# A two-layer hybrid diffusion step with an expert mixture: gate products among key transposes, another order of the routing, and one expert transfer with a place of its own

## What is computed

```python
def block(x, mod, lp, ctx=None):
    sh1, sc1, g1, sh2, sc2, g2 = jnp.split(mod, N_MOD, axis=-1)
    h = rmsnorm(x, lp['norm1_g']) * (1 + sc1) + sh1
    y, new = token_mixing(h, lp, ctx)        # pooling, banded attention, latent attention; gated, merged, projected
    x = x + g1 * y
    h = rmsnorm(x, lp['norm2_g']) * (1 + sc2) + sh2
    x = x + g2 * ec_moe(h, lp['w_router'], lp['w_gate'], lp['w_up'], lp['w_down'])
    return x, new

def ec_moe(h, w_router, w_gate, w_up, w_down):
    b, n, d = h.shape
    cap = CAPACITY_FACTOR * n // N_EXPERTS   # 16 slots for the prompt, 32 for the latents, 16 experts
    aff = jax.nn.softmax(jnp.einsum('bnd,de->ben', h, w_router), axis=1)
    vals, idx = lax.top_k(aff, cap)
    xg = jax.vmap(lambda hb, ib: hb[ib])(h, idx)
    a = jnp.einsum('becd,edf->becf', xg, w_gate)
    u = jnp.einsum('becd,edf->becf', xg, w_up)
    o = jnp.einsum('becf,efd->becd', jax.nn.silu(a) * u, w_down) * vals[..., None]
    return jax.vmap(lambda ib, ob: jnp.zeros((n, d), ob.dtype).at[ib.reshape(-1)].add(ob.reshape(-1, d)))(idx, o)
```

## Time and profile before

| what | value |
|---|---|
| median of 3 runs | 1815.55 us (1815.0 to 1815.77) |
| the profiled execution | 1816.19 us |
| its span on the core | 1814.3 us |
| TensorE busy | 1702.5 us, 94% |
| VectorE, ScalarE, GpSimd busy | 650.5, 288.4, 118.5 us |
| DMA | 533.81 MB, mean 294 GB/s |
| expert transfers | 192 of 2048 KB, 31.6 and 30.6 us from issue to landing |
| granted TensorE clock, mean | 0.998 |

### The profile page before, as it was taken

How to read it: one execution, slowest core, us unless ns; L and a number is a source line. 1 busy time by engine, 2 the same in 40 slices (tenths; PEclk the granted TensorE clock), 3 DMA queues, 4 the chain that set the end, 5 groups by cost and what they waited for, 6 DMA issues and landing times.

```text
span 1814.3 us, 18937 instructions
## 1 busy us (share of the span) xinstructions
PE 1702.5 (94%) x7152; PEld 801.6 (44%) x7152; DVE 650.5 (36%) x1381; ACT 288.4 (16%) x733; POOL 118.5 (7%) x160
## 2 busy tenths in 40 slices
PE   6998999999999998898899989999999999988987
PEld 2455566654434333242245555666543433323322
DVE  1345655567212210221124466555661221211211
ACT  2233322111100010000022432221021000000000
POOL 1151000000000000000012500000000000000000
PEclk9999999999999999999999999999999999999999
DMA  9430333754899999999983213337648999999997
GB/s 383 178 122 24 116 116 116 278 200 182 356 429 432 431 430 432 430 431 429 429 359 119 99 47 116 116 128 294 234 189 359 429 430 431 431 431 431 430 431 315
DMA packets 49106, 533.81 MB, mean 294 GB/s; under 512 B 5840, under 2 KB 6896, under 8 KB 10384
## 3 DMA queue, kind: packets, MB, share of 16 engines
q1 hardware_dynamic: 45776, 524.39, 69.8%
q0 software_dynamic: 2112, 7.97, 1.2%
q10 hardware_dynamic: 1152, 0.56, 0.1%
HBM read 530.76 MB, written 2.13 MB: 294 GB/s over the span
## 4 chain that ended last, share of the span: by engine, by line
PE 72%; DMA 23%; DVE 3%; ACT 1%; issue 1%; SPq 0%; ACTq 0%; POOL 0%; DVEq 0%; POOLq 0%
PE bank L1957 21%; DMA ring<-in_w_moe 21%; PE bank L1583 12%; PE bank L1602 7%; PE bank L1648 6%; PE bank L1994 5%; PE bank L1819 5%; PE bank L1684 2%; DMA ring<-in_w_mix 2%; PE bank L1886 2%; PE bank L1745 2%; PE bank L1611 1%; PE bank L1720 1%; PE bank L1626 1%; PE bank L1571 1%; PE bank L1574 1%
## 5 line engine op out<-in xcount | busy, mean ns | idle before, releaser
L1583 PE MATMUL bank<-hT,ring 128*128 128x384 f32 x768 | 258.6, 490 | 0.0
L1957 PE MATMUL bank<-M,hT 128*64 128x512 f32 x1024 | 228.8, 595 | 21.0 <-DMA M<-in_w_moe 19.8
L1957 PE MATMUL bank<-ring,hT 128*64 128x512 f32 x1024 | 227.2, 595 | 11.4 <-DMA ring<-in_w_moe 11.4
L1583 PEld LDWEIGHTS bank<-hT,ring 128*128 128x128 f32 x768 | 143.4, 190 | 103.4 <-issue 7.8
L1957 PEld LDWEIGHTS bank<-M,hT 128*64 128x64 f32 x1024 | 72.5, 137 | 167.8 <-issue 136.8
L1957 PEld LDWEIGHTS bank<-ring,hT 128*64 128x64 f32 x1024 | 72.2, 137 | 158.2 <-issue 139.7
L1602 PE MATMUL bank<-M,ring 128*128 128x384 f32 x384 | 134.6, 494 | 5.6 <-ACT M L760 5.6
L1957 PE MATMUL bank<-ring,M 128*64 128x512 f32 x512 | 115.4, 596 | 18.7 <-DMA ring<-in_w_moe 18.7
L1957 PE MATMUL bank<-M 128*64 128x512 f32 x512 | 115.7, 595 | 12.3 <-DMA M<-in_w_moe 12.3
L1648 PE MATMUL bank<-ring,hT 128*128 128x512 f32 (+1 forms) x288 | 117.4, 567 | 2.8 <-DVE hT L1051 2.1
L951 ACT ACTIVATE hT<-bank 128x512 f32<-128x512 f32 x32 | 19.1, 598 | 571.6 <-PE bank L1957 571.6
(11 more groups left out here) (236 smaller groups left out, 1536.8 us busy)
## 6 DMA issues: line engine op xcount, KB each, us to landing
M<-in_w_moe SPq DMA_DIRECT2D x96, 2048.0 KB, 31.6
ring<-in_w_moe SPq DMA_DIRECT2D x96, 2048.0 KB, 30.6
ring<-in_w_mix SPq DMA_DIRECT2D x110, 1024.0 KB, 5.1
ring<-in_w_mix SPq DMA_DIRECT2D x4, 576.0 KB, 4.9
modrow<-in_bias_rows POOLq DMA_DIRECT2D x4, 512.0 KB, 5.7
g2slot<-in_bias_rows POOLq DMA_DIRECT2D x4, 512.0 KB, 7.3
M<-in_counts POOLq DMA_DIRECT2D x2, 768.0 KB, 12.4
out<-x SPq DMA_DIRECT2D x6, 256.0 KB, 2.0
```

Of the source, the lines that this page charges most:

```text
L1583: ins = mm(ps[:, 0:TOK], w[:, q, (j % 4) * P:(j % 4 + 1) * P], hT[:, 4 * h + q, :], start=(h == 0 and q == 0), stop=(h == 1 and q == 3))
L1957: ins = mm(bank[b][64 * e:64 * e + 64, :], lhs(e, 4 * h + q), w[:, q, :], start=(h == 0 and q == 0), stop=(h == 1 and q == 3))
```

## The change

It has four parts. First, `wq` products run tile by tile with both halves, in other banks; ScalarE issues the cache stores after the evacuation of `tq`; key transposes `tkm` get other banks, and `gate(0, 0)` stands between the second and third of them, its tanh ahead of the first exponentials. Head pair 0 is written out: both branch products, the second gate and the transposed probabilities follow in a new order, and VectorE merges the first branch ahead of its first `divide`. Second, `column(6)` to `column(8)` come at head pairs 2, 4 and 6 instead of 3, 5 and 7. Third, routing: `turned(0, 0)` moves from VectorE to ScalarE, `router_part(0)` ahead of `normal_x(2)`, `route(0)` ahead of the last gate row, and bank 2's gather ahead of `turn_slots(1)`. Fourth, the small arrays move into one buffer `arena` of two units; once attention and most of routing have read them, transfer j = 16 of the last group (pair 7, its transfer 4) is loaded there, right behind the ring's first fill, and the ring's own transfer is left out. The order of unit pairs becomes 0, 4, 2, 6. `wrout` is cleared at each layer's start.

```diff
@@ -30 @@
 EARLY = (8, 10, 12)
-DOUBLES = EARLY + (0, 2, 4, 6) + (14,)
+DOUBLES = EARLY + (0, 4, 2, 6) + (14,)
 ND = len(DOUBLES)
@@ -139 @@
         for t in range(T):
-            use(("wq", h, t), 1 + 3 * h + t)
+            use(("wq", h, t), 1 + 2 * t + h)
     for g in range(4):
@@ -150 @@
         for h in range(2):
-            use(("tkm", t, h), ((3, 4), (5, 0), (7, 4), (1, 2))[t][h])
+            use(("tkm", t, h), ((7, 0), (3, 4), (3, 4), (5, 6))[t][h])
     for m in range(NM):
...
             use(("sb", m, j), 2 * j + 1)
-        if m in (3, 5, 7):
-            use(("col", 6 + (m - 3) // 2), 5)
+        if m in (2, 4, 6):
+            use(("col", 5 + m // 2), 5)
         for j in range(2):
@@ -229 @@
 LANDED = [sum(slot_of(u) == s for u in UNITS) for s in range(RINGX)]
-LANDS = [c + (12 * NP // ND if s % 2 == 0 else 0) for s, c in enumerate(LANDED)]
+LANDS = [c + (12 * NP // ND - (s == DOUBLES[16 % ND]) if s % 2 == 0 else 0) for s, c in enumerate(LANDED)]
 SUMMED = (6, 7, 8, 9, 4, 5, 10, 11)
@@ -268 @@
         ring = sb("ring", [P, RING, UNIT])
-        kT = sb("kT", [P, 512])
+        M = sb("M", [P, 20160])
+        arena = sb("arena", [P, 2 * UNIT])
+        kT = arena[:, 1024:1536]
         cols = sb("cols", [P, L, NCOL])
-        rows = sb("rows", [P, NROW])
+        rows = arena[:, 1536:1536 + NROW]
         const = sb("const", [P, NCONST])
         cs = sb("cs", [P, KB, 32])
-        modrow = sb("modrow", [P, 2, 512])
+        modrow = arena[:, 0:1024].rearrange("p (a b) -> p a b", b=512)
         shift = [sb(f"shift{k}", [P, KB, 2]) for k in range(2)]
...
         g2slot = sb("g2slot", [P, D])
-        wrout = sb("wrout", [P, KB, 32])
-        kr = sb("kr", [P, 4, ROPE])
-        krg = sb("krg", [P, 4, ROPE])
+        wrout = arena[:, 3016:3272].rearrange("p (a b) -> p a b", b=32)
+        kr = arena[:, 3272:3400].rearrange("p (a b) -> p a b", b=ROPE)
+        krg = arena[:, 3400:3528].rearrange("p (a b) -> p a b", b=ROPE)
         sskr = sb("sskr", [P, 4])
@@ -287 @@
         rcon = sb("rcon", [P, 2, NE])
-        wrA = sb("wrA", [P, 2, KB, 32])
+        wrA = arena[:, 2504:3016].rearrange("p (s a b) -> p s a b", a=KB, b=32)
         negsink = sb("negsink", [P, SH])
@@ -296 @@
 
-        M = sb("M", [P, 20160])
 
@@ -379 @@
         landed = [sem(f"landed{s}") for s in range(RINGX)]
+        resident_in = sem("resident_in")
         first_half_used = sem("first_half_used")
@@ -547 @@
 
-            def load_group(l, gr, first):
+            def load_resident(l):
+
+                wait_full(sp, l, ("rpart", 0))
+                wait_full(sp, l, ("modb", 10, 0))
+                sp.dma_start(arena[:, :], a["w_moe"][l, NP - 1, 4]).then_inc(resident_in, 16)
+
+            def load_group(l, gr, first, last=False):
                 for j in range(len(EARLY) if first else 0, 24):
                     s = DOUBLES[j % ND]
+                    if last and j == 16:
+                        continue
+                    if first and j == ND:
+                        load_resident(l)
                     if j >= ND:
@@ -576 @@
                 load_group(l, 0, True)
-                with sp.Fori(1, NG) as gr:
+                with sp.Fori(1, NG - 1) as gr:
                     load_group(l, gr, False)
+                load_group(l, NG - 1, False, True)
             for n in range(2):
@@ -591 @@
             step(nc.gpsimd.memset(mhalf[:, :], -0.5))
-            nc.gpsimd.memset(wrout[:, :, :], 0.0).then_inc(pads_zero, 1)
             events = [0]
@@ -602 @@
             for l in range(L):
-                if l == 0:
-                    pool.wait_ge(pads_zero, 1)
-                else:
+                if l > 0:
                     x_final(pool, l - 1)
+                nc.gpsimd.memset(wrout[:, :, :], 0.0).then_inc(pads_zero, 1)
+                pool.wait_ge(pads_zero, l + 1)
                 loads = [
@@ -802 @@
 
-                for dst, src, s in ((outs[2][0, l], ktok[:, 0, :], ktok_ready), (outs[3][0, l], vtok[:, 0, :], None),
-                                    (outs[4][0, l], ckvtok[:, 0, :], ckvtok_ready), (outs[5][0, l], kr[:, 0, :], None)):
-                    if s is not None:
-                        act.wait_ge(s, 3 * l + 1)
-                    act.dma_start(dst, src).then_inc(cache_out, 16)
-
                 for t in range(T):
@@ -826 @@
                     read(l, ("tq", t), F(qT[:, :, t * P:(t + 1) * P], ps[:, :].rearrange("p (b t) -> p b t", t=P), ACT.Copy))
+
+                for dst, src, s in ((outs[2][0, l], ktok[:, 0, :], ktok_ready), (outs[3][0, l], vtok[:, 0, :], None),
+                                    (outs[4][0, l], ckvtok[:, 0, :], ckvtok_ready), (outs[5][0, l], kr[:, 0, :], None)):
+                    if s is not None:
+                        act.wait_ge(s, 3 * l + 1)
+                    act.dma_start(dst, src).then_inc(cache_out, 16)
 
@@ -852 @@
 
+                gate_tanh(l, 0, 0)
                 for j in range(2):
@@ -863 @@
                     for j in range(2):
-                        gate_tanh(l, (2 * m + j) // 8, (2 * m + j) % 8)
+                        if m:
+                            gate_tanh(l, (2 * m + j) // 8, (2 * m + j) % 8)
+                        elif j == 0:
+                            gate_tanh(l, 0, 1)
                         if j == 0 and m not in (0, 4):
@@ -916 @@
                 expert_exp(2)
+                turned(0, 0)
                 wait_full(act, l, ("wo", 1, 0))
...
                 turned(0, 1)
+                router_part(0)
                 normal_x(2)
-                router_part(0)
                 expert_exp(0)
@@ -1298 @@
                 for m in range(NM):
+                    if m == 0:
+                        merge(l, 0, 0)
                     for j in range(2):
                         divide(l, m, j)
-                    if m in (3, 5, 7):
-                        column(6 + (m - 3) // 2)
-                    merge(l, m // 4, 2 * m % 8)
+                    if m in (2, 4, 6):
+                        column(5 + m // 2)
+                    if m:
+                        merge(l, m // 4, 2 * m % 8)
                     for j in range(2):
...
                             sum_rows(6 + m // 2, m % 2, (0, 1))
-                    merge(l, m // 4, 2 * m % 8 + 1)
+                            if m == 0:
+                                merge(l, 0, 1)
+                    if m:
+                        merge(l, m // 4, 2 * m % 8 + 1)
                     if m + 1 < NM:
@@ -1427 @@
                 number(P, TOK)
-                turned(0, 0)
                 add_mixed(1, 0)
@@ -1711 @@
                     wait_read(pe, l, ("tkc", t))
-                for h in range(2):
-                    arrived(l, ("wq", h, 0))
-                    w = ring[:, slot_of(("wq", h, 0)), 0:3 * QR].rearrange("p (k n) -> p k n", n=QR)
-                    for t in range(T):
+                    for h in range(2):
+                        arrived(l, ("wq", h, 0))
+                        w = ring[:, slot_of(("wq", h, 0)), 0:3 * QR].rearrange("p (k n) -> p k n", n=QR)
                         ps = begin(l, ("wq", h, t))
@@ -1748 @@
 
-                for t in range(4):
+                for t in range(2):
+                    turn_heads("tkm", t, 3 + t)
+                gate(l, 0, 0)
+                for t in (2, 3):
                     turn_heads("tkm", t, 3 + t)
@@ -1756 @@
                     wait_read(pe, l, ("pool", g))
+
                 def column(i):
@@ -1777 @@
                     b, j = m // 4, 2 * m % 8
+                    if m == 0:
+                        branch(l, 0, 0)
+                        gate(l, 0, 1)
+                        turn_probs(l, 0, 0)
+                        branch(l, 0, 1)
+                        turn_probs(l, 0, 1)
+                        scores(l, 1)
+                        continue
                     gate(l, b, j)
-                    if m not in (0, 4):
+                    if m != 4:
                         values(l, m - 1)
-                    if m in (3, 5, 7):
-                        column(6 + (m - 3) // 2)
+                    if m in (2, 4, 6):
+                        column(5 + m // 2)
                     branch(l, b, j)
@@ -1926 @@
                 router(0)
+                route(0)
                 gate_row(11, 1)
-                route(0)
                 pe.wait_ge(xn2_ready, 3 * l + 2)
...
                 turn_affinities(1, 0, 1)
-                gather_sample(0, (1,))
+                gather_sample(0, (1, 2))
                 turn_slots(1, 0, 1)
-                gather_sample(0, (2, 3))
+                gather_sample(0, (3,))
                 pe.wait_ge(xn2_ready, 3 * l + 3)
@@ -1950 @@
                         s = DOUBLES[j % ND]
-                        pe.wait_ge(landed[s], 16 * (l * LANDS[s] + LANDED[s] + gr * (24 // ND) + j // ND + 1))
+                        resident = last and j == 16
+                        if resident:
```

(7 more changed lines are left out.)

## The result

The changed kernel took 1797.46 us (median of 4 runs, 1796.35 to 1798.8) against 1815.66 (4 runs, 1815.0 to 1816.09) beside it: a ratio of 0.9901 (95% interval 0.9885 to 0.9916), 18.2 us less. The forecast was 1790.9: the sign and the range held, and the kernel came out 6.6 us above it.

A forecast was written before the change was run, and what follows sets the result against it. Transfers bound the expert stages, TensorE attention and routing. Per layer 5.4 (attention) + 2.9 (routing) + 4.9 (resident transfer), twice 26.4, less 1.7 for a clock fall: 24.7 us saved, median 1790.9 us, range 1785.7 to 1799.

The forecast's parts named there:

- Attention, up to the third gate product: Attention: TensorE waits of 8.1 us per layer go, a new 2.7 comes; net 5.4 per layer, bounds 3 to 6.3.
- The stores: Attention's cache stores: issued later, they take 5.2 us to land, still before the first key/value evacuation; no cost.
- The new wait: Attention, before the second gate: TensorE idles 2.7 us per layer until VectorE's merge frees bank 7.
- the clock fall behind it: After the 2.7 us idle before the second gate: one fall counted in the two layers, costing 1.7 us.
- The column products: Attention, one head pair earlier: may wait up to 0.6 us, cover other small tanh waits (2.0 in two layers); net 0.
- Rival (c): Second gate in attention: its wait grows, clock falls in both layers, 1.5 us more idle each; 1795.6 us, chance 0.10.
- Routing: Between attention and experts: 0.5 us from earlier logits plus 2.4 from fewer gather records, 2.9 per layer, bounds 1.5 to 3.3.
- Resident transfer: Expert stage: one transfer leaves the stream, loaded while DMA would be idle; 4.9 us per layer, bounds 0 to 5.3.
- Rival (d): Expert stream: new memory places lower its rate; slower than before under 417.6 GB/s, 1832.7 us at 410; chance 0.03.
- The signs listed as wrong: Transfer rate under 425 GB/s, first reuse waiting behind the resident transfer, or experts starting under 6 us earlier.
- the experts' start in layer 0: Sign of success: layer 0's expert products start 8.3 us earlier, near 458.6 us.
- the end of layer 0's stream: Sign of success: layer 0's expert stage is over 13 us earlier.

The follow-up runs named there:

- the kernels with the early merge: Changed kernel with the first merge between the two first maxima and columns back at head pairs 3, 5, 7: 1788.88 us; with M also at its old address: 1783.86 us.
- the two edits of before: Kernel before with small arrays in the arena, nothing loaded there, M behind: 1821.9 us; kernel before with M directly behind the ring: 1819.05 us.
- the last kernel: Changed kernel with the first merge between the first maxima, columns back at head pairs 3, 5, 7, and M at its old address: 1783.86 us, ratio 0.9823.

## Why the prediction was right, and where it was not

**Attention, up to the third gate product: right, and too small.** The waits that were to go went. From the start of the last transposes ahead of `wq` (`tq`) to the start of the third gate product before had 112.81 to 178.92 and after 113.79 to 173.07, 6.8 us less; the idle listed in between fell from 8.06 in seven waits to 2.55 in one, only 5.5. The other 1.3 hangs on the waits too. Groups without a wait between them overlap in the timeline. PE, layer 0, before:

```profile
139.53 1.04 PE L1739 MATMUL bank<-const,M 128*96 128x128 f32 x8
140.40 3.60 PE L1745 MATMUL bank<-ring,M 128*128 128x512 f32 x8
```

The first ends, by the profile, 0.17 after the second starts. Behind a wait there is no such overlap, so each of the six waits that went gave some 0.16 beyond its listed idle, 1.0 in all. The last 0.3 is in groups that were listed longer behind a wait (3.70 against 3.60 for a key/value product, 1.08 against 1.04 for a key transpose).

The stores landed in 1.7 us where the earlier trace rows has 5.2; that size was wrong and cost nothing. DMA issues of after:

```profile
out<-arena ACTq DMA_DIRECT2D x2, 16.0 KB, 1.7
```

In before the DMA engines were busy with other transfers while the stores were under way (a share of 0.91 to 1.02 from 110 to 116 us in layer 0); in after the first store went out at 115.3, and from 116 to 118 us the share was 0.51. The Trainium skill (DMA: Bandwidth & Descriptors, Anatomy of one DMA) gives about 2 us as the fixed cost of a transfer issued by GpSimd. These stores are ScalarE's; the row of after is near that figure, and that of before is not.

**The new wait: right** (2.55 for 2.7), and so was the clock fall behind it: in after it came in one of the two layers, and it cost 1.6 for 1.7.

**The column products: wrong at nothing.** The wait of up to 0.6 was in the bounds (0.67), but the step "they cover the other small tanh waits: 0" missed the clock. Behind the short wait and the 1.9 us of one-column products it fell in both layers of after, 1.6 us each. The two were not tried apart, but neither was followed by a fall alone: none came behind the column products of after at head pairs 4 and 6, which had no wait, nor behind the 0.65 us wait of the kernels with the early merge. Without falls attention would have given 6.9 and 7.0 per layer, 1.5 more than the forecast 5.4; three falls of 1.6 took 4.8 of 13.9, and 9.1 is left. That this equals the forecast 2 x 5.4 - 1.7 is luck: a gain that was put too small and two falls that were not foreseen cancel. Rival (c) has its falls here, but in another place than it said.

**Routing: right, in sum and in its parts** (2.80 and 2.99 for 2.9). In layer 0 the slot transposes came 55.21 us after the output projection's start instead of 55.67, 0.5 as forecast, and 8 records of 1.13 stand behind them instead of 16 of 3.55, the forecast 2.4. Of these 2.4, 1.5 is the clock (3.55 against 2.05 in the layer in which it held); before pays that in some executions only.

**Resident transfer: right** at 5.0 for 4.9, a price that was read straight off the stream.

**The rate: the step that failed.** Rival (d) named the mechanism, M starting elsewhere, and priced only the size at which it would turn the sign, under 417.6 GB/s; for the sum it counted nothing, "nothing in the rows". What the runs show in the place of that nothing is 0.6%, 431 to 428 GB/s, 2.4 us per layer (428.9 against 426.5), 4.8 in all. The signs listed as wrong ("under 425") would not have caught it either. A cost that no row shows should have had both ends in the sum: each 1% on the 857 us of streamed transfers is 8.6 us, a third of the whole forecast. Of the signs, the experts' start in layer 0 came 7.1 us earlier (466.92 to 459.79) for the forecast 8.3, and the end of layer 0's stream 9.7 earlier (898.25 to 888.51), where over 13 had been named: that sign failed, by the rate and by the program's start.

The account against the forecast, profile to profile: 24.7 forecast, 19.25 measured. Experts 9.8 - 5.1 = 4.7 short (rate 4.8), attention and routing 0, the start of the program 1.0, the rest -0.2. That start goes with M's address too, at least in part, since DMA is never idle there: from 6 to 40 us it moved 410 to 412 GB/s in the five profiled executions that have M at its old address and 403 to 406 in the nine others. In executions without a clock fall at the start, the first long group begins at 46.0 to 46.7 with M at its old address and at 46.8 to 47.2 with M elsewhere; in four others the clock fell there, and it begins at 47.8 to 49.0. The last 1.1 us to the medians is that the forecast took before's median as 0.64 below its profile, while after's is 0.52 above.

**Left open.** Why M's address matters is not known: two other addresses were held against the old one (directly behind the ring, and 2272 bytes above the old), and no alignment or boundary was tested by itself. In the built programs M starts at byte 145920 of a partition where the stream runs at 431 GB/s, a multiple of 512; the addresses with 428, 118912 and 148192, are no multiples of 256. That is the property to try first. In the two edits of before other arrays moved with M, though none that the stream writes; in the last kernel the small arrays stay away from their old places and the rate is back, which speaks for M alone.

## What to carry to other kernels

In a stage that streams without a gap, compare the rate to three digits before and after any edit of the memory layout, and put an array that the stream fills back at its old address before you judge the edit; 0.6% of an 860 us stream is 5 us, as much as one whole transfer of 2 MB. When a wait moves to another engine's queue, look at what stands ahead of the releasing instruction there: one merge put ahead of one block of maxima gave 1.8 us per layer, and no clock fall came behind what was left of its wait in the four layers measured. Count clock falls one by one, since an edit that is right can look worthless in the medians when a fall moves elsewhere.

## What the runs showed of the hardware that was not expected

- The transfer rate of a stream from HBM depended on where in memory one of its two target tiles lies: 431 GB/s at one address of M, 428 at two others, with the same transfers.
- The clock fell to 1.2 GHz behind an idle of 2.55 us in 7 of the 12 layers that had it, and behind 0.67 us of idle with 1.92 us of one-column products after it in 8 of the 10 layers that had those. Each fall cost some 1.6 us. It comes and goes between executions: in routing of the kernel before, layer 1 had it in one profiled execution and not in another.
- A wait of PE costs more than its listed idle, since groups without a wait overlap by some 0.16 us in the timeline: six waits with 5.5 us of idle between them gave 6.8 when they went.
